# Long convolutions of an encoder layer: from a radix-4 VectorE stage with dense class transforms to two TensorE stages with a reordering by DMA between them

## The reference, cut to what matters

```
kern = kern * lax.rsqrt(jnp.sum(jnp.square(kern), axis=0, keepdims=True))
kspec = jnp.fft.rfft(kern, axis=0)
def long_conv(z, ks, d):
    zf = jnp.fft.rfft(z, n=2 * L, axis=1)
    return jnp.fft.irfft(zf * ks[None], n=2 * L, axis=1)[:, :L] + d * z
z = x1 * long_conv(v, kspec[:, 0], bias[0])
return x2 * long_conv(z, kspec[:, 1], bias[1])
```

## Time and profile before

| | |
|---|---|
| median of three runs | 2903.33 us |
| profiled execution: span | 2904.9 us |
| long convolutions: first DMA to the next phase's first DMA | 908.4 to 1280.8 us |
| whole kernel, busy: PE / DVE / ACT / POOL | 2493.5 / 1342.0 / 730.4 / 426.9 us |
| TensorE's mean granted clock | 0.925 |

### The profile page before, as it was taken

The page is one execution under the profiler, slowest core; times in us unless marked ns, Lnnn a source line. Parts: engine busy times, 40 slices in busy tenths (PEclk is TensorE's granted clock), DMA queues, the critical chain, the costliest instruction groups (busy, mean ns, idle before and its releaser), DMA issues. The chain is left out here.

```text
span 2904.9 us, 27922 instructions
## 1 busy us (share of the span) xinstructions
PE 2493.5 (86%) x10860; PEld 2004.6 (69%) x10860; DVE 1342.0 (46%) x1518; ACT 730.4 (25%) x1016; POOL 426.9 (15%) x335
## 2 busy tenths in 40 slices
PE   5999999827986978938877879999999999499898
PEld 4888888604764867825655657888888888378686
DVE  4232221168686999955453353333333333322432
ACT  4222221132221211225441241212122221221321
POOL 0000000004442877721000000000000000000000
PEclk9999999957998999969988979999999999799999
DMA  3222222130116211152204411111111110534542
GB/s 125 73 80 72 71 74 84 58 105 19 62 69 221 73 58 58 55 181 71 85 25 149 152 52 48 51 69 51 58 51 58 61 53 34 157 99 115 149 139 83
DMA packets 164890, 242.88 MB, mean 84 GB/s; under 512 B 6823, under 2 KB 124455, under 8 KB 163656
## 3 DMA queue, kind: packets, MB, share of 16 engines
q1 hardware_dynamic: 153560, 192.21, 21.1%
q0 software_dynamic: 10096, 46.40, 4.4%
q10 hardware_dynamic: 1152, 3.15, 0.3%
HBM read 173.84 MB, written 67.90 MB: 83 GB/s over the span
## 5 line engine op out<-in xcount | busy, mean ns | idle before, releaser
L128 PE MATMUL up_acc<-up_h_hi,up_w_hi 128*128 128x512 f32 x1056 | 411.9, 390 | 3.1 <-DVE up_w_lo L474 3.1
L129 PE MATMUL up_acc<-up_h_lo,up_w_hi 128*128 128x512 f32 x1056 | 411.5, 390 | 0.0
L130 PE MATMUL up_acc<-up_h_hi,up_w_lo 128*128 128x512 f32 x1056 | 411.5, 390 | 0.0
L245 DVE SCALAR_TENSOR_TENSOR up_u<-up_acc,up_conv_par,up_u 128x1023 f32<-128x1023 f32 x88 | 85.4, 1012 | 462.8 <-ACT up_u L462 462.8
L128 PE MATMUL in_acc<-in_h_hi,in_w_hi 128*128 128x512 f32 x696 | 273.6, 393 | 3.1 <-DVE in_w_lo L343 3.1
L129 PE MATMUL in_acc<-in_h_lo,in_w_hi 128*128 128x512 f32 x696 | 272.0, 391 | 0.0
L130 PE MATMUL in_acc<-in_h_hi,in_w_lo 128*128 128x512 f32 x696 | 271.9, 391 | 0.0
L128 PE MATMUL down_acc<-down_w_hi,down_s_hi 128*128 128x512 f32 x528 | 209.8, 397 | 52.7 <-DVE down_w_lo L640 40.1
L128 PEld LDWEIGHTS up_acc<-up_h_hi,up_w_hi 128*128 128x128 f32 x1056 | 198.8, 188 | 44.7 <-issue 3.4
L129 PEld LDWEIGHTS up_acc<-up_h_lo,up_w_hi 128*128 128x128 f32 x1056 | 198.8, 188 | 41.3
L130 PEld LDWEIGHTS up_acc<-up_h_hi,up_w_lo 128*128 128x128 f32 x1056 | 198.7, 188 | 41.3
(11 more groups left out here) (221 smaller groups left out, 4141.0 us busy)
## 6 DMA issues: line engine op xcount, KB each, us to landing
down_s_raw<-g_scratch SPq DMA_DIRECT2D x24, 1408.0 KB, 6.8
up_w_raw<-arg_w_up_t SPq DMA_DIRECT2D x44, 512.0 KB, 3.6
g_scratch<-up_prod POOLq DMA_DIRECT2D x22, 768.0 KB, 3.5
in_w_raw<-arg_w_in_t SPq DMA_DIRECT2D x29, 512.0 KB, 3.7
tok_scratch<-in_out POOLq DMA_DIRECT2D x16, 768.0 KB, 4.9
out_s_raw<-y_scratch SPq DMA_DIRECT2D x24, 512.0 KB, 3.8
down_w_raw<-arg_w_down_t SPq DMA_DIRECT2D x22, 512.0 KB, 4.3
k_scratch<-filt_kout SPq DMA_DIRECT2D x8, 1024.0 KB, 3.9
```

Source lines behind the costliest of these rows:

```text
L128: pe.matmul(out, w_hi, x_hi, start=first, stop=False)
L129: pe.matmul(out, w_hi, x_lo, start=False, stop=False)
L130: return pe.matmul(out, w_lo, x_hi, start=False, stop=last)
L245: dve.scalar_tensor_tensor(u[:, t0 + 1:t0 + n], acc[:, t0:t0 + n - 1], w_prev, u[:, t0 + 1:t0 + n], ALU.mult, ALU.add).then_inc(half_step, 1)
```

## The change

The four classes per job become radix(s) classes: 16 for the long sequence, 8 for the short one, each of 64 positions. There are four streams (sequence, half), 24 token tiles of 128 in all, and 48 pairs of classes over both orders. For each stream and order:

- split: per token tile two matmuls with a small table (`otab`) make real and imaginary parts of all classes; ScalarE copies them to `split`.
- `shuffle_classes`: DMAs from SBUF to SBUF bring `split` (partition = position within a group and class) to `classes` (partition = real or imaginary and position, class along the free dimension). One DMA for each tile b and part ri: 128 partitions of 1 KB in, q = 128 / radix partitions out (8 for the long sequence, 16 for the short).
- pair: `forward` is two matmuls, `multiply` is one VectorE operation of 1024 elements per partition that reads PSUM and a spectrum pair (present twice, in partitions 0 to 63 and 64 to 127), `inverse` is four matmuls, and ScalarE copies back into `classes`.
- `shuffle_split`: the same DMAs the other way.
- turn: per tile two matmuls join, VectorE scales and adds (`finish`), and TensorE either splits the tile for the second order or transposes it for the store. GpSimd prepares z times bias times gate and gate times scale ahead of it.

One hand-written `schedule` sets the order on all engines; `turn_after` says behind which pair each turn comes. SP issues every load and every shuffle in that order, spectra three pairs ahead (`ring`). The filters store the spectra in runs of 1 KB. The 1/sqrt of the filters' power is taken on a [128, 16] tile and goes through DRAM (`scale_d`).

```
--- before.py
+++ after.py
                     sp.wait_ge(k_copied, (j + 1) * CLASSES)
-                    sp.dma_start(k_d[s][o, half, :, ri, :, :, :], kout[j % 2][:, :, 0:sns[s], :]).then_inc(k_stored[j % 2], 16)
+                    sp.dma_start(k_d[s][o, :, ri, :, half * HC:(half + 1) * HC].rearrange("(c k) p e -> p c k e", c=CLASSES),
+                                 kout[j % 2][:, :, 0:sns[s], :]).then_inc(k_stored[j % 2], 16)
                     if j % per_group == 0:
...
+SUB = 64
+def radix(s):
+    return SEQS[s][1] // SUB
+def spectral_classes(s):
+    if radix(s) == 16:
+        return [(c4, c4 + 8) if kb == 0 else (7 - c4, 15 - c4) for c4 in range(CLASSES) for kb in range(2)]
+    return [(c4, 7 - c4) for c4 in range(CLASSES)]
...
+    outer = np.zeros((P, 4, P), np.float32)
+    for j, w in enumerate((np.cos(phi), -np.sin(phi))):
+        for i in range(q):
+            outer[i::q, j, i * r:(i + 1) * r] = w
+            outer[i * r:(i + 1) * r, 2 + j, i::q] = w.T
...
+    streams = [(s, half) for s in range(len(SEQS)) for half in range(2)]
+    nbs = [n // P for _, n in SEQS]
+    n_tiles = [len(spectral_classes(s)) for s in range(len(SEQS))]
+    pairs = [(o, st, t) for o in range(ORDER) for st, (s, _) in enumerate(streams) for t in range(n_tiles[s])]
+    final_pair = {(o, st): max(g for g, (oo, ss, _) in enumerate(pairs) if (oo, ss) == (o, st))
+                  for o in range(ORDER) for st in range(len(streams))}
+    lag, ring = 2, 3
+    turns = [(o, st) for o in range(ORDER) for st in range(len(streams))]
+    turn_after = {(0, 0): 14, (0, 1): 21, (0, 2): 25, (0, 3): 29, (1, 0): 38, (1, 1): 45, (1, 2): 49, (1, 3): 49}
+    schedule = [("split", 0, st) for st in range(len(streams))]
+    for g in range(len(pairs) + lag):
+        schedule.append(("pair", g, None))
+        schedule += [("turn", o, st) for o, st in turns if turn_after[o, st] == g]
...
+        split = [p.sb(f"split{st}", [P, nbs[s], 2, HC]) for st, (s, _) in enumerate(streams)]
+        classes = [p.sb(f"classes{st}", [P, radix(s), HC]) for st, (s, _) in enumerate(streams)]
+        kf = [p.sb(f"kf{b}", [P, 2, 2, HC]) for b in range(ring)]
+        prod = [p.sb(f"prod{b}", [P, 2, 2, HC]) for b in range(2)]
...
+        def tile_rows(s, first, width, b):
+            t0, n = SEQS[s]
+            return mix_d.rearrange("t p c -> (t p) c")[t0:t0 + n, first:first + width].rearrange(
+                "(a b m) c -> b a m c", a=radix(s), b=nbs[s])[b]
...
+                def load_k(g):
+                    o, st, t = pairs[g]
+                    s, half = streams[st]
+                    for dup in range(2):
+                        for u in range(2):
+                            sp.dma_start(kf[g % ring][dup * SUB:(dup + 1) * SUB, u, :, :],
+                                         k_d[s][o, t, :, u * SUB:(u + 1) * SUB, cols(half)].rearrange("r j e -> j r e")
+                                         ).then_inc(k_loaded[g % ring], 16)
+                def load_gate(i):
+                    o, st = turns[i]
+                    s, half = streams[st]
+                    for b in range(nbs[s]):
+                        sp.dma_start(gate[i % 2][:, b, :], tile_rows(s, o * HY + half * HC, HC, b)).then_inc(gate_loaded[i % 2], 16)
+                    at = (s * ORDER + o) * HY + half * HC
+                    sp.dma_start(rows[i % 2][:, 0, :], scale_d[at:at + HC].rearrange("(a n) -> a n", a=1).broadcast_to([P, HC])
+                                 ).then_inc(gate_loaded[i % 2], 16)
+                    sp.dma_start(rows[i % 2][:, 1, :], hy_bias[o:o + 1, cols(half)].broadcast_to([P, HC])).then_inc(gate_loaded[i % 2], 16)
+                def shuffle_classes(o, st):
+                    s, half = streams[st]
+                    q = P // radix(s)
+                    for b in range(nbs[s]):
+                        sp.wait_ge(sem["v_copied"], v_before[o, st] + b + 1)
+                        for ri in range(2):
+                            at = ri * SUB + q * b
+                            sp.dma_start(classes[st][at:at + q, :, :], split[st][:, b, ri, :]).then_inc(to_classes[st], 16)
+                def shuffle_split(o, st):
+                    s, half = streams[st]
+                    q = P // radix(s)
+                    sp.wait_ge(sem["g_copied"], final_pair[o, st] + 1)
+                    for b in range(nbs[s]):
+                        for ri in range(2):
+                            at = ri * SUB + q * b
+                            sp.dma_start(split[st][:, b, ri, :], classes[st][at:at + q, :, :]).then_inc(to_split[st], 16)
+                for s in range(len(SEQS)):
+                    sp.dma_start(otab[s][:, :, :], outer_tab[s]).then_inc(sem["otab_loaded"], 16)
+                for b in range(nbs[0]):
+                    sp.dma_start(z[0][:, b, :], tile_rows(0, 2 * HY, HY, b)).then_inc(z_loaded[0][b], 16)
...
+                for b in range(nbs[1]):
+                    sp.dma_start(z[1][:, b, :], tile_rows(1, 2 * HY, HY, b)).then_inc(z_loaded[1][b], 16)
+                sp.dma_start(tab[0][:, :, :, :, :], inner_tab[0]).then_inc(tab_loaded[0], 16)
+                for g in range(ring):
+                    load_k(g)
+                sp.dma_start(tab[1][:, :, :, :, :], inner_tab[1]).then_inc(tab_loaded[1], 16)
+                sp.wait_ge(sem["inverted"], 1)
+                sp.dma_start(scale_d.rearrange("(p x) -> p x", p=P), power[:, :]).then_inc(sem["scale_stored"], 16)
+                for kind, at, st in schedule:
+                    if kind == "split":
+                        shuffle_classes(0, st)
+                        if st == 1:
+                            sp.wait_ge(sem["scale_stored"], 16)
+                            load_gate(0)
+                            load_gate(1)
+                    elif kind == "pair":
+                        if at + ring < len(pairs):
+                            sp.wait_ge(sem["multiplied"], at + 1)
+                            load_k(at + ring)
+                        for o, other in turns:
+                            if final_pair[o, other] + lag == at:
+                                shuffle_split(o, other)
+                    else:
+                        if at == 0:
+                            shuffle_classes(1, st)
+                        i = turns.index((at, st))
+                        if i + 2 < len(turns):
+                            sp.wait_ge(sem["z_ready"], y_before[turns[i + 1]])
+                            load_gate(i + 2)
...
+                def split_tile(o, st, b):
+                    s, half = streams[st]
+                    v = v_before[o, st] + b
+                    if o == 0:
+                        pe.wait_ge(z_loaded[s][b], 16)
+                    else:
+                        pe.wait_ge(sem["z_ready"], y_before[0, st] + b + 1)
+                    if v >= 2:
+                        pe.wait_ge(sem["v_copied"], v - 1)
+                    for ri in range(2):
+                        last = pe.matmul(vacc[v % 2][:, ri, :], otab[s][:, ri, :], z[s][:, b, cols(half)], start=True, stop=True)
+                    last.then_inc(sem["v_ready"], 1)
                 def forward(g):
...
+                    o, st, t = pairs[g]
+                    s, _ = streams[st]
+                    if t == 0:
+                        pe.wait_ge(tab_loaded[s], 16)
+                        pe.wait_ge(to_classes[st], 32 * nbs[s] * (o + 1))
+                    if g >= 2:
+                        pe.wait_ge(sem["multiplied"], g - 1)
+                    for u, c in enumerate(spectral_classes(s)[t]):
+                        last = pe.matmul(xacc[g % 2][:, u, :], tab[s][:, t, u, 0, :], classes[st][:, c, :], start=True, stop=True)
+                    last.then_inc(sem["x_ready"], 1)
                 def inverse(g):
...
+                    o, st, t = pairs[g]
+                    s, _ = streams[st]
+                    pe.wait_ge(sem["multiplied"], g + 1)
+                    if g >= 2:
+                        pe.wait_ge(sem["g_copied"], g - 1)
+                    for u in range(2):
+                        for i in range(2):
+                            last = pe.matmul(gacc[g % 2][:, u, :], tab[s][:, t, u, 1 + i, :], prod[g % 2][:, u, i, :],
+                                             start=i == 0, stop=i == 1)
+                    last.then_inc(sem["g_ready"], 1)
+                def join_tile(o, st, b):
+                    s, _ = streams[st]
+                    y = y_before[o, st] + b
+                    if b == 0:
+                        pe.wait_ge(to_split[st], 32 * nbs[s] * (o + 1))
+                    if y >= 2:
+                        pe.wait_ge(sem["z_ready"], y - 1)
+                    for ri in range(2):
+                        last = pe.matmul(yacc[y % 2][:, 0:HC], otab[s][:, 2 + ri, :], split[st][:, b, ri, :],
+                                         start=ri == 0, stop=ri == 1)
+                    last.then_inc(sem["y_ready"], 1)
...
```

(114 more changed lines are left out.)

344 lines of the change are left out of this document (96 added, 248 removed).

## The result

The changed kernel takes 3009.9 us (median of 4 runs, 2989.8 to 3028.2) against 2905.0 us before (4 runs, 2901.7 to 2907.7): a ratio of 1.036, 95% interval 1.031 to 1.041. The sign, the mechanism and the place were right; the size of the main term was not. The profiled execution is the slowest of the four, 3028.2 us with a span of 3026.6, so the profile shows 123 us of loss, 18 more than the median. One of the eleven runs of the later schedule (run e9) took 3353 us at a lower clock and is left out of its median; its trace is the only one of that kernel.

The account below looks back on a forecast made before the run. VectorE's `stage` and `end` work was taken to bound the phase. 1052.5 to the fourth spectrum + 122.4 pairs + 91.8 turns + 229 stalls + 4.4 gave 1500, 219 us after 1280.8, so 3122 us; range 2865 to 3210.

Parts of the forecast that it names:

- What bounds the phase, and that only its end counts: Convolution phase: held by VectorE's `stage` and `end` work; the change is worth what its end at 1280.8 us moves by.
- The matmul work: TensorE in the convolution phase: 480 matmuls at 0.453 us, 217 us; 2.72 us per pair; saves about 108 us busy.
- rival B: Shuffles run at the rate of 64-partition loads, 10 us long and 5 short; phase ends 1226, time 2849; chance 0.20.
- named this and left it out: Matmuls after idle time start at half speed: up to 2 us for each of eight gaps, left out as small.
- VectorE: Pairs and turns: `multiply` 1.22 us, `finish` two operations of 0.42 us per tile, 99 us in all, covered by TensorE.
- GpSimd, the stores, the conversions: Side work: GpSimd's three operations 20 us per turn, covered; filters' 1 KB stores taken as 0; sqrt through DRAM free.
- a long shuffle of 40 us: Long stream's shuffle, 2.1 MB with 8 partitions on one side: 52 GB/s taken, 40 us; 31 to 45 had chance 0.55.
- The sum with the measured sizes: Forecast's phase sum: fourth spectrum at 1052.5, pairs 122.4, turns 91.8, stalls 229, last 4.4; end at 1500 us.
- Smaller terms that were off and cancelled: On the queue before the fourth spectrum pair: two gates 8 us, two short shuffles 20 us.
- rival C: Neighbouring DMAs overlap fully, long shuffle 20 us, time 2926; break-even about 17 us; chance 0.17 including what lies around it.
- The rule of the Trainium skill: Shuffle DMAs: rate follows ports reached; 8 partitions have 2 ports, 54 GB/s, 2.4 us; sum some 10 us less.
- The signs named: Expected in the profile: 16 issues about 40 us, `multiply` waiting over 150 us for `conv_kf`, TensorE's groups about 228 us.

Follow-up runs that it names:

- e9: Turns two or three pairs later and short streams split behind pairs 4 and 6, on the kernel with partitions four apart and fewer spectra DMAs: 2906.3 us, 1.000.
- e12: Kernel with each shuffle DMA's partitions four apart, loading only the first three pairs' spectra: 2837.5 us, 0.978.
- e11: The changed kernel, neighbouring partitions kept, loading only the first three pairs' spectra: 2911.9 us, 1.004.
- e8: The changed kernel with only the order of a long stream's shuffle DMAs changed, those 32 partitions apart following each other: 3079.5 us, 1.060.
- wide kernel: The changed kernel with shuffles of the same bytes and number of DMAs between 128 partitions on both sides, reordering left out: 2892.6 us, 0.996.
- e3: The changed kernel with the shuffles issued from GpSimd's queue instead of SP's, partitions as in the change: 2974.3 us, 1.023.

## Why the prediction was right in direction and wrong in size

- **What bounds the phase, and that only its end counts**: held. The time followed the moment of the next phase's first DMA: 1403.7, 1278.9 (spread), 1212.2 us (spread, no spectra), and in each the profiled execution ends 1623 to 1625 us behind it.
- **The matmul work**: held for the pairs, not for the sum of all groups. A pair takes 2.59 us undisturbed (2.72 forecast). With fast shuffles and no spectra the phase ended at 1212, near the 1226 of rival B. TensorE's groups add to 281 us, not 228 (256 us by the stages, where overlapping records count once). I had priced every matmul at 0.453 us; those of `inverse` took 0.48, those of `forward`, split and join 0.57 to 0.71. Its granted clock is 0.74 on the mean, where the earlier trace rows show 0.95: 0.50, the lower of its two levels, in the stretch 955 to 975 us without work. I had named this and left it out. How much of the difference the clock makes isn't shown: the same matmuls are busy 242 us at 0.88 in e12 and 237 at 0.81 in e11.
- **VectorE**: the multiply takes 1.225 us as forecast; the second operation of `finish` takes 0.74 us, not 0.42, so the three groups add to 115 us instead of 99. It is covered, as forecast.
- **GpSimd, the stores, the conversions**: covered, as forecast; a long turn's three GpSimd operations take 13.5 us, not 20.
- **The step that failed: a long shuffle of 40 us.** It took 30.0 us to the classes and 22.6 to 24.0 back, below even the 31 to 45 that the forecast stood for. I had put 52 GB/s, between 26 in proportion to the earlier trace rows and 210, and stayed near the proportional line because both known points lie on it. They are rows of single loads with half of the partitions; the small DMAs behind each other in a queue brought more than I granted, and by direction: 70 GB/s writing few partitions, 89 reading them. Another order alone (e8) took a `shuffle_split` to 30 us and the whole time 70 us up.
- **The sum with the measured sizes.** 942 + 60 + 8 + 20 + 2.5 = 1032.5 for the fourth spectrum (it came at 1039.0); stalls 4 x (23.5 + 4.5 - 8.2) = 79, then 17 and 25 for the two of order 1, and 13, 5, 5 as they were: 144 instead of 229. 1032.5 + 122.4 + 91.8 + 144 + 4.4 = 1395, 105 us less than the 1500 of the prediction and 8.6 short of the 1403.7 of the trace. Of the 105, 20 are the first two shuffles, 65 the four splits, 20 the two to the classes. So the model of what waits for what was good in sum and the one size fed into it was too large by a third in one direction and by 70% in the other. Single stalls were less good: in the trace `multiply` waits 23.8, 18.4, 26.8 and 24.3 us behind the four splits, where the sum has 19.8, and 27.4 and 16.7 behind the two long shuffles of order 1, where it has 17 and 25.
- **Smaller terms that were off and cancelled, by luck**: the two first gates took SP 21 us (993.3 to 1014.5) instead of 8, and the first two short shuffles 5.2 us each in their issues instead of 10. The gates' runs of 1 KB are not the reason: behind spread shuffles the same issues take 12.4 us (968.7 to 981.2). They follow right behind the two slow shuffles on the queue; what exactly held them isn't shown.
- **The break-even of rival C.** A long shuffle of 17 us was to decide the sign. With 15.0 and 10.4 us (spread) the kernel is 6 us faster than before. The same sum with these sizes, 12.5 us of gates and 10.3 of short shuffles: 942 + 30 + 12.5 + 10.3 + 2.5 = 997.3, stalls 4 x 6.7 + 2 + 10 + 4 + 5 + 5 = 53, end 1269; measured 1278.9.
- **The rule of the Trainium skill.** By the Trainium skill's page SBUF — State Buffer (Door 1: The DMA port swizzle) four neighbouring partitions share a port, and the rate follows how many ports a DMA's partitions reach. The spread version agrees: 8 partitions, 4 apart, give 2.0 to 2.7 times the rate of 8 neighbours. The estimate worked out from that page, 54 GB/s for 8 neighbours, was below both measured rates (70 and 89). By the rule for the number of engines on the Trainium skill's page DMA: Bandwidth & Descriptors (Why a DMA increments its semaphore by 16 and not by 1), a DMA of 128 partitions on one side and 8 on the other runs on 8 of the 16. The shares, 0.46 to 0.57, lie around the 0.50 that this would give; they are means over 16 engines and don't show which were busy.
- **The signs named**: `multiply` for `conv_kf` first and over 150 us (213), TensorE's `forward` for `multiply` (75.6), SP held in its shuffles, no PE share over 85% (256 of 497 us): all there. Three signs didn't show: 16 issues in about 40 us, about 50 GB/s, and TensorE's groups at about 228 us.

## What to carry to other kernels

A DMA between SBUF partitions is priced by which partitions its narrow side touches: eight neighbours gave 70 to 89 GB/s, the same eight 4 apart 181 to 191, for nothing but a permuted table. When a change trades engine work for shuffles on a queue that also feeds the engines, price the queue first, and price both what stands behind the shuffle and what waits for the shuffle itself: taking away the neighbours alone brought 110 us, the spectra's loads alone 98, both together 172. The rate extrapolated from single loads was here too low for a stream of small DMAs, by a third in one direction and 70% in the other, so a forecast whose sign hangs on it deserves a wide range.

## What the runs showed of the hardware that I had not expected

- Reading few neighbouring partitions is faster than writing them (23.5 against 30.0 us for 2.1 MB), and in the one other order that was run only reading became slower (30 to 33 us when those 32 apart follow each other).
- SP issued the shuffles' DMAs at best every 0.64 us (16 in 10.3 us in the wide kernel, in 10.4 in the spread one), so with 16 of them a long shuffle has a floor of 10 us that no choice of partitions lowered; the earlier trace rows had 0.52 us for the spectra's.
- Two kernels with shuffles of neighbouring partitions spread by 38 and 44 us between runs (the changed kernel, and the one with fewer spectra DMAs); those with spread partitions by 7 to 16, the kernel before by 5 to 8. Why stays open: three others with neighbours spread by only 7 (e8), 16 (e3) and 23 us (e11), and with 4 to 10 runs of each the figures are rough.
